# Modulation sums moved from GpSimd to VectorE, and a layer's high parts multiplied ahead of its low parts

## The reference, cut to what matters

```
cond = silu(c)                                        # 1024 numbers
for i in range(4):
    shift, scale, gate = split(cond @ ada_w[i] + ada_b[i], 3)    # ada_w[i]: 1024 x 3072
    h = rmsnorm(x, norm_g[i]) * (1 + scale) + shift
    y = mixer_i(h)            # h @ w_in, attention, (o * silu(gate')) @ w_out
    x = x + gate * y
```

## Time and profile before

| | us |
|---|---|
| median of 3 runs | 2717.4 (2715.82 to 2725.14) |
| profiled execution | 2716.97 |
| its span, first to last instruction | 2715.2 |
| PE busy | 2407.9 (89%) |
| PEld busy | 1833.5 (68%) |
| DVE busy | 1598.5 (59%) |
| ACT busy | 765.6 (28%) |
| POOL busy | 915.3 (34%) |
| mean granted TensorE clock | 0.921 of full speed |

### The profile page before, as it was taken

The page is one execution under the profiler, slowest core; times in us unless marked ns, Lnnn a source line. Parts: engine busy times, 40 slices in busy tenths (PEclk is TensorE's granted clock), DMA queues, the critical chain, the costliest instruction groups (busy, mean ns, idle before and its releaser), DMA issues.

```text
span 2715.2 us, 31261 instructions
## 1 busy us (share of the span) xinstructions
PE 2407.9 (89%) x12233; PEld 1833.5 (68%) x12233; DVE 1598.5 (59%) x2435; ACT 765.6 (28%) x1706; POOL 915.3 (34%) x944
## 2 busy tenths in 40 slices
PE   3969898788999899799969989999998997999988
PEld 2756676567987666677747776577677685757666
DVE  7786674763235566664664557674745445958373
ACT  2233202512001355224331233221402215232231
POOL 2873897387800345781120010401302001040030
PEclk6979898798678899899989999999999999999999
DMA  6440455044543100441011211121121121213111
GB/s 213 140 132 8 117 135 129 1 116 117 127 78 62 32 1 3 123 116 63 32 58 59 71 48 63 32 78 63 47 93 63 62 63 33 62 47 93 47 62 62
DMA packets 229157, 200.27 MB, mean 74 GB/s; under 512 B 86835, under 2 KB 213139, under 8 KB 228755
## 3 DMA queue, kind: packets, MB, share of 16 engines
q1 hardware_dynamic: 217491, 156.33, 20.6%
q0 software_dynamic: 11520, 41.95, 5.2%
HBM read 196.16 MB, written 2.10 MB: 73 GB/s over the span
## 4 chain that ended last, share of the span: by engine, by line
PE 57%; POOL 17%; DVE 17%; ACT 5%; issue 3%; DMA 0%; SPq 0%; DVEq 0%; ACTq 0%; POOLq 0%
PE bank L506 13%; PE bank L507 13%; PE bank L508 13%; POOL mix L2220 6%; POOL mix L2217 4%; PE bank L618 4%; DVE wring_parts L1515 3%; PE bank L654 3%; POOL mix L2223 2%; PE bank L632 2%; POOL mix L2204 2%; DVE whi_parts L1514 2%; PE bank L818 2%; DVE qb L1959 1%; PE bank L572 1%
## 5 line engine op out<-in xcount | busy, mean ns | idle before, releaser
L507 PE MATMUL bank<-h_parts,whi_parts 128*128 128x512 f32 (+2 forms) x1336 | 539.5, 404 | 0.0
L1515 DVE TENSOR_TENSOR wring_parts<-wring,whi_parts 128x2048 fp32r<-128x2048 f32 (+1 forms) x138 | 326.4, 2365 | 4.7
L1514 DVE CAST whi_parts<-wring 128x2048 fp32r<-128x2048 f32 (+1 forms) x138 | 192.3, 1394 | 201.5 <-PE bank L508 167.1
L507 PEld LDWEIGHTS bank<-h_parts,whi_parts 128*128 128x128 f32 (+2 forms) x1336 | 253.6, 190 | 69.2 <-issue 5.9
L2220 POOL TENSOR_TENSOR mix<-mix 128x512 f32<-128x512 f32 (+1 forms) x160 | 214.5, 1341 | 12.5
L506 PE MATMUL bank<-vt_parts,whi_parts 128*128 128x512 f32 (+2 forms) x472 | 199.9, 424 | 18.1 <-POOL h_parts L2251 12.1
L507 PE MATMUL bank<-mix_parts,whi_parts 128*128 128x512 f32 x512 | 202.9, 396 | 0.0
L506 PE MATMUL bank<-pt_parts,whi_parts 128*128 128x512 f32 x392 | 166.3, 424 | 36.7 <-DVE wring_parts L1515 20.9
L508 PE MATMUL bank<-vt_parts,wring_parts 128*128 128x512 f32 (+2 forms) x472 | 190.4, 403 | 0.0
L1586 DVE CUSTOM_DVE_ANT_0 bank<-bank,causal 128x128 f32<-128x128 f32 (+3 forms) x256 | 120.2, 512 | 76.0 <-PE bank L618 75.6
L618 PE MATMUL bank<-kb,qb 64*128 64x128 f32 (+3 forms) x1024 | 156.7, 385 | 8.7 <-ACT pr L1199 4.0
(11 more groups left out here) (375 smaller groups left out, 5363.9 us busy)
## 6 DMA issues: line engine op xcount, KB each, us to landing
wring<-in_w_in SPq DMA_DIRECT2D x60, 1024.0 KB, 5.2
mix<-in_ada_w POOLq DMA_DIRECT2D x80, 512.0 KB, 4.6
wring<-in_w_out SPq DMA_DIRECT2D x16, 1024.0 KB, 5.1
wring<-in_mla_w_in SPq DMA_DIRECT2D x10, 1024.0 KB, 7.0
wring<-in_mla_w_out SPq DMA_DIRECT2D x8, 1024.0 KB, 5.2
wring<-in_swa_w_in SPq DMA_DIRECT2D x32, 256.0 KB, 4.7
wring<-in_nsa_w_in SPq DMA_DIRECT2D x32, 256.0 KB, 4.5
wring<-in_nsa_w_in SPq DMA_DIRECT2D x6, 1024.0 KB, 5.2
```

The lines of the kernel that those rows point to most:

```text
L507: pe.matmul(bank, lh, rl, start=False, stop=False)
L1514: chain(dve.tensor_copy(high, whole))
L1515: dve.tensor_tensor(low, whole, high.bitcast(F32), ALU.subtract).then_inc(done, 1)
```

## The change

GpSimd's sums go. Its `ada_loads` starts the loads alone: a load is now two row chunks of 512 columns (512 KB as before), and from the third on it waits until the rows of the load two before are summed. VectorE's `ada_rows(more)` sums the next rows as `weighted_rows` does, one 128 by 512 instruction a row, 16 rows a part, 160 in all; it is called behind gates (4 rows each in layer 0, else 2), behind the q ropes of layers 1 and 2 (2 each) and behind the residuals of y0 to y4 (3, 3, 3, 3, 4) in layers 0 to 2. The modulation of part 3L+4 moves on TensorE from behind y7 to ahead of y6, and on VectorE to ahead of `residual(L, 6)`. `tables(1)` moves behind the `prepare` that follows `constants()`. `first_blocks` makes the four products with the high part of h as soon as this is there, and the two with the low part two chunks later (LOW_LAG). It holds for all six layers.

```diff
...
 AHEAD = 2
+LOW_LAG = 2
...
                 b = [open_bank(A, key) for key in keys]
-                for k in range(KC):
-                    right = hk(k)
-                    for j in range(2):
-                        mm = product(b[j][:, :], [t[:, k, j * P:(j + 1) * P] for t in by_chunk(slots)], right, k == 0, k == KC - 1)
-                        if k == KC - 1:
-                            mm.then_inc(A.full, 1)
+                unseen[0] = 0
+                for step in range(KC + LOW_LAG):
+                    if step < KC:
+                        pe.wait_ge(*cnt(h_kept))
+                        for j in range(2):
+                            high, low = [t[:, step, j * P:(j + 1) * P] for t in by_chunk(slots)]
+                            pe.matmul(b[j][:, :], high, hh[step], start=(step == 0), stop=False)
+                            pe.matmul(b[j][:, :], low, hh[step], start=False, stop=False)
+                    k = step - LOW_LAG
+                    if k >= 0:
+                        pe.wait_ge(*cnt(h_ready))
+                        for j in range(2):
+                            high = by_chunk(slots)[0][:, k, j * P:(j + 1) * P]
+                            mm = pe.matmul(b[j][:, :], high, h_parts[:, k, :], start=False, stop=(k == KC - 1))
+                            if k == KC - 1:
+                                mm.then_inc(A.full, 1)
...
-                pe.wait_ge(*(cnt(start_summed, 2) if n < 2 else cnt(ada_summed)))
+                pe.wait_ge(*(cnt(start_summed, 2) if n < 2 else (ada_step, 2 * KC * (n - 1))))
                 bank = open_bank(V, ("ada", L, part))
...
                 for i in range(4):
+                    if L + 1 < len(LAYERS) and i == 3:
+                        modulation(L + 1, 1)
                     keys = [(L, "y", 2 * i + j) for j in range(2)]
...
                 out_proj(L, 1)
-                if L + 1 < len(LAYERS):
-                    modulation(L + 1, 1)
             norm_x(4)
...
+            summed = [0]
+
+            def ada_rows(more):
+
+                for _ in range(more):
+                    n, at = divmod(summed[0], 2 * KC)
+                    half, k = divmod(at, KC)
+                    u, n = KC * (n + 2) + at // 2, n + 2
+                    summed[0] += 1
+                    if k % 2 == 0:
+                        dve.wait_ge(ada_loaded[u % 2], 16 * (u // 2 + 1 - KC))
+                    t = ada_ring[:, u % 2, S * (k % 2):S * (k % 2 + 1)]
+                    to = acc[:, n % 2, S * half:S * (half + 1)]
+                    if k == 0:
+                        dve.wait_ge(*V.filled(("ada",) + todo[n - 2]))
+                        dve.tensor_scalar(to, t, cond[:, 0:1], None, ALU.mult).then_inc(ada_step, 1)
+                    else:
+                        dve.scalar_tensor_tensor(out=to, in0=t, scalar=cond[:, k:k + 1], in1=to, op0=ALU.mult, op1=ALU.add).then_inc(ada_step, 1)
+                    dve.wait_ge(*cnt(ada_step))
+
             def tables(source):
...
                 chain(dve.tensor_reduce(inv[:, :], invsel[:, :], AX.X, ALU.add))
-                tables(1)
...
                         gate((L, "gate", b), mix[:, b, :])
+                        ada_rows(2 if L else 4)
                         if b == 1 and L:
...
                     if L == 0:
+                        tables(1)
                         dve.wait_ge(*cnt(tables_act, 3))
...
                         rope((L, "q", b), scale)
+                        ada_rows(2)
                         if b % 2:
                         gate((L, "gate", b), mix[:, b, :])
+                        ada_rows(2)
                         if b in (1, 3):
...
                         rope((L, "q", b), scale)
+                        ada_rows(2)
                         if b % 2:
...
                             gate((L, "gate", 2 * i + j), mix[:, 2 * i + j, :])
+                            ada_rows(2)
                         if i < 2:
...
                 for b in range(KC):
+                    if b == 6 and L + 1 < len(LAYERS):
+                        modulation(L + 1, 1)
                     residual(L, b)
                         prepare()
+                    if b < 5 and L + 1 < len(LAYERS):
+                        ada_rows(3 if b < 4 else 4)
                 add_square(L + 1, KC - 1)
                 prepare()
-                if L + 1 < len(LAYERS):
-                    modulation(L + 1, 1)
             norm_apply(4, lambda k: col("final_norm_g", k), x, x_normed)
...
-            def modulation(n):
...
+            asked = [2 * KC]
+
+            def ada_loads(n, ahead):
+
+                for u in range(asked[0], min(KC * n + ahead, KC * len(todo))):
+                    L, part = todo[u // KC]
+                    w = a["ada_w"][L].rearrange("(k p) n -> p k n", p=P)
+                    k, c = 2 * (u % 4), part * D + S * (u % KC // 4)
+                    if u >= 2 * KC + 2:
+                        pool.wait_ge(ada_step, 2 * (u - 2 * KC - 1))
+                    pool.dma_start(ada_ring[:, u % 2, :].rearrange("p (k n) -> p k n", k=2), w[:, k:k + 2, c:c + S]).then_inc(ada_loaded[u % 2], 16)
+                    asked[0] = u + 1
...
                 low_parts(L)
-                modulation(3 * L + 2)
-                if L + 1 < len(LAYERS):
-                    modulation(3 * L + 3)
+                ada_loads(3 * L + 4, 2)
                 if LAYERS[L] == "nsa":
...
                 normalise(L)
-                if L + 1 < len(LAYERS):
-                    modulation(3 * L + 4)
+                ada_loads(3 * L + 5, 2)
...
```

More of the change, by code:

```diff
@@ L241, in mix_high @@
             return [qb_parts[:, k, :] for k in range(KC)]
+        todo = [(L, part) for L in range(len(LAYERS)) for part in range(3)]
         def squares_of(n):
@@ L267, in program @@
         gate_done = sem("gate_done")
-        cond_tanh, cond_ready, ada_step, ada_summed = sem("cond_tanh"), sem("cond_ready"), sem("ada_step"), sem("ada_summed")
+        cond_tanh, cond_ready, ada_step = sem("cond_tanh"), sem("cond_ready"), sem("ada_step")
         small_normed, lat_split = sem("small_normed"), sem("lat_split")
@@ L2194, in _ @@
             pool.iota(pcol[:, :], [[0, 1]], base=0, channel_multiplier=1).then_inc(consts_ready, 1)
-            todo = [(L, part) for L in range(len(LAYERS)) for part in range(3)]
-            parts_done = []
-            def ada_load(n, r):
-                L, part = todo[n]
-                u = KC * n + r
-                w = a["ada_w"][L].rearrange("(k p) n -> p k n", p=P)
-                c = part * D + r * P
-                pool.dma_start(ada_ring[:, u % 2, :].rearrange("p (k n) -> p k n", k=KC), w[:, :, c:c + P]).then_inc(ada_loaded[u % 2], 16)
@@ L2206, in modulation @@
-            def modulation(n):
-                if n == 2:
-                    ada_load(2, 0)
-                    ada_load(2, 1)
-                    pool.wait_ge(*cnt(cond_ready))
-                pool.wait_ge(*V.filled(("ada",) + todo[n - 2]))
-                for r in range(KC):
-                    u = KC * n + r
-                    t = ada_ring[:, u % 2, :].rearrange("p (k n) -> p k n", k=KC)
-                    pool.wait_ge(ada_loaded[u % 2], 16 * (u // 2 + 1 - KC))
-                    pool.tensor_tensor(t, t, cond[:, :, None].to_broadcast([P, KC, P]), ALU.mult).then_inc(ada_step, 1)
-                    for width in (4, 2):
-                        pool.wait_ge(*cnt(ada_step))
-                        pool.tensor_tensor(t[:, 0:width], t[:, 0:width], t[:, width:2 * width], ALU.add).then_inc(ada_step, 1)
-                    pool.wait_ge(*cnt(ada_step))
-                    last = ada_summed if r == KC - 1 else ada_step
-                    pool.tensor_tensor(acc[:, n % 2, r * P:(r + 1) * P], t[:, 0], t[:, 1], ALU.add).then_inc(last, 1)
-                    pool.wait_ge(*cnt(last))
-                    nn, rr = (n, r + 2) if r < KC - 2 else (n + 1, r + 2 - KC)
-                    if nn < len(todo):
-                        ada_load(nn, rr)
```

## The result

The changed kernel takes 2695.0 us (median of 4 runs, 2693.7 to 2697.1) against 2717.5 before; ratio 0.9917, 95% interval 0.9899 to 0.9934. It is faster by 22 us, less than half of the 51 forecast; the time lies inside the range. The span of the profiled execution went from 2715.2 to 2693.8 us, TensorE's mean granted clock from 0.921 to 0.928. One execution of the experiment mod_last ran in a slow state (3226.9 us at a granted clock of 0.68) and is left out of its ratio; its median without it is 2672.7 us.

The account below looks back on a forecast made before the run. GpSimd was taken to cost twice: TensorE waits for its modulation sums, and it slows VectorE beside it. Terms 21 + 4 + 17 + 9 + 8 - 11 = 48, plus 3 allowance: 2717 - 51 = 2666 us; 8-in-10 range 2644 to 2698.

Parts of the forecast that it names:

- (b): First blocks, high parts first: products start 1.9 us sooner; 4 us (0 to 5) counted for the second stack's two layers.
- (a): Layer 0 ahead of attention: quiet VectorE and tables moved behind kv_b's split start attention at 175.5 instead of 196.53, 21 us.
- (c): Tails of layers 0, 1, 2: waits ahead of the norm go, less small products and a 3 us stall; 17 us (14 to 27).
- (d): Layer 1 ahead of attention: TensorE's 8.87 us wait for GpSimd goes; 9 us, 4 if splits come late.
- (e): Layer 3 ahead of attention: VectorE's ropes and splits run at quiet durations, TensorE's clock stays up; 8 us (3 to 8).
- (f): Layer 2: a loss, softmax maskings queue on GpSimd behind loads that wait for rows; -11 us (-6 to -14).
- allowance: VectorE's other stretched splits, in layer 0's last attention unit and layer 2's first blocks: 3 us, between 0 and 6.
- Rival 1: The two-slot load ring starves VectorE: each us of landing over 4.6 costs 17 us, up to 2763 us; chance 0.05.
- rival 2: The tails give little: a stall of 8 us instead of 3 makes 2681; chance 0.20, together with smaller gains up to 2709.

Follow-up runs that it names:

- mod_last: Also experiment 1: the changed kernel with the modulation put back behind y7, the rows staying where they are; 2673.3 us, ratio 0.9845.
- experiment 2: Also rows_ahead: the changed kernel, modulation still mid-tail, four of its sixteen rows summed earlier, ahead of attention's last output unit; 2677.7 us, ratio 0.9856.
- Experiment 3: The changed kernel with each load of modulation rows after the first two bringing 128 instead of 512 columns; 2676.7 us, ratio 0.9838.
- experiment 6: The changed kernel, layer 0 only: key blocks copied out ahead of sine and cosine, last two query swaps behind the value blocks; 2697.9 us, ratio 0.9942.
- experiment 5: Also tables_back: the changed kernel with VectorE's table work back ahead of kv_b's split in layer 0; 2701.8 us, ratio 0.9936.
- experiment 7: The changed kernel with the first two blocks of each layer in the order of the kernel before; 2708.6 us, ratio 0.9981.
- gps_busy: The changed kernel with twelve extra GpSimd multiplications on a dead buffer, in layer 0's tail and ahead of layer 1's attention; 2720.6 us, single execution.
- combined: The changed kernel with modulation behind y7, layer 2's loads between maskings, layer 0's key blocks copied ahead of sine and cosine; 2665.0 us, ratio 0.9808.
- experiment 4: The changed kernel with GpSimd's loads in layer 2 issued between its maskings, the last two behind the last masking; 2694.0 us, ratio 0.9924.

## Why the prediction was wrong

Direction and range were right, the size was not: 22 us (21.4 in the spans) for 51. By its own steps, in us; (b)'s share of other layers lies in (a) and (c), as in the prediction:

| step | forecast | measured |
|---|---|---|
| (a) layer 0 ahead of attention | 21 | 11.3 |
| (b) first blocks, second stack | 4 | 0.2 |
| (c) tails of layers 0 to 2 | 17 | 3.5 |
| (d) layer 1 ahead of attention | 9 | 7.7 |
| (e) layer 3 ahead of attention | 8 | 6.9 |
| (f) layer 2 | -11 | -8.9 |
| allowance; attention of layers 0, 1, 3 and the rest | 3 | 0.7 |

(The measured (c) is -4.0 in the tails and 2.8 + 2.8 + 1.9 from the norm to the next first product: 9.53 us before in all three, now 6.70, 6.70 and 7.65. (d), (e) and (f) count from that product.)

**The step that failed is (c)**, in the sentence "Paid: the modulation's 16 small products stand in the middle of TensorE's work, 1.84 us at full clock, and TensorE waits there for row 16." The stall was sized right, 3.6, 3.8 and 3.7 us against 3 (0 to 4). Its price was not. I let TensorE resume at full speed; after the stall the products took 3.57 us and y6's first twelve products ran at half speed, a clock of 0.76 over 18 us. Three times 1.7 and 2.7 us (experiment 2) are 13.2, against the 13.5 that (c) falls short. The rows to see it in were before me: 3.80 us of waiting and then 2.30 us for the same products, 10.76 and then 3.57, and the 0.65 of the earlier trace rows. Experiments 1 and 2 show both halves: leave the products where they are but without a stall, and the tails are 7.7 to 9.1 us shorter; put them behind y7, and it is 1.7 more. The same term explains why the tail of layer 0 got slower than before (56.8 for 53.3), although a 3.80 us wait ahead of the norm had gone: it was traded for one in the middle of the work.

The Trainium skill, "TensorE: Matmul & The Clock Gate", in its section on HAM oscillation, describes that rule: a wait lets the gate throttle TensorE, and what comes next starts cold. The trace agrees: 3.57 us for the products behind the wait of 3.60, 1.84 without one. The prediction reckoned with it for the norm's product and not for this place.

**(a), second in size.** kv_b's split ended 5.2 us late: the first gate ran at 98.2 instead of 96, and VectorE's waits for loads, put at 2.5 us for each of four pairs, 10, were 13.8. The other 4.5 us lie behind the split. Experiment 3 prices the waits: with 7.2 us of them attention starts at 177.7, 2.2 from the forecast. Another part is ScalarE: sine and cosine stood between TensorE and its banks (the 5.28 us wait), while the prediction let the copies follow them without holding TensorE; experiment 6 gave 3.4 to 4.2 back. The tables' move itself is worth nothing (experiment 5). The two small modulations stand in series in front of attention with 3.63 us.

**(b).** In the first stack the 1.9 us show as 0.7 to 2.2 ahead of each attention (experiment 7). In the second stack the first blocks did end earlier, by 0.8 us in layer 4 and 1.6 in layer 5, 2.4 for the forecast's 4; the clock behind them undid it. Layer 5 takes 673.4 us from its norm to the end for 670.0 before and 669.9 in the old order. That is no chance of one execution: from layer 5's first norm to its second, all twelve profiles with the new order take 375.6 to 375.7 us and both with the old one 372.1 to 372.2. Layer 4 took 668.6 us from norm to norm for 672.3 before and 672.7 in the old order, but four of the twelve with the new order (rows_ahead, tables_back, gps_busy, combined) took 671.4 to 672.0, so most of that gain is not the order's.

Most of layer 5's loss can be seen behind one wait of TensorE. First the kernel after, time line and the 20 us from the wait's end, then the one with the old order:

```profile
2337.70 3.68 PE L1009 MATMUL bank<-ident,qb 128*128 128x128 f32 x16 [3.03 <-DVE qb L2009]
```

```profile
2337.70:2357.70 20.00, 19.89 (x64) 13.43 (x65) 13.47 (x35) 3.51 (x9) 6.71 (x8) 0.78 0.00 1
```

```profile
2355.40 3.29 PE L999 MATMUL bank<-ident,qb 128*128 128x128 f32 x16 [3.03 <-DVE qb L1999]
```

```profile
2355.40:2375.40 20.00, 19.92 (x73) 12.56 (x74) 13.66 (x35) 5.63 (x14) 7.63 (x9) 0.93 0.11 30
```

The same wait of 3.03 us, and a clock of 0.78 in one and 0.93 in the other. Why an edit far ahead of it changes the clock there is open.

**Right** were the price of a row (0.78 us from start to start, four in 3.11), the quiet durations, (d), (e), and (f) with its mechanism, 8.9 us for 11; experiment 4 gave 4.5 to 5 us of it back. Rival 1 had the right place, the ring, with a smaller effect; rival 2 named the right stage and priced it by the stall alone.

## What to carry to other kernels

A wait of TensorE in the middle of dense work can cost the wait and, behind it, time at half clock: here 3.7 us of waiting with sixteen small products behind it cost 8 to 9, and behind a wait of 1.62 us with full products after it the clock stayed up. Price it from rows of the same kind, and put an operand that comes late where TensorE waits anyway. Before a chain is moved off one engine, follow the ring that feeds it: VectorE waited 13.8 us for loads ahead of layer 0's attention, and what was queued behind the loads in layer 2 cost another 4.5 to 5.

## What the runs showed of the hardware

GpSimd's arithmetic costs VectorE its own duration, one to one, where an instruction of VectorE that has its operands in SBUF (seen for the split's subtraction and the ropes) falls beside it: 18.7 us for 19.1. In the kernel before the cast and the gates grow too (1.23 to 2.34 us for the cast, ahead of layer 1's attention). An instruction that reads a bank ran beside GpSimd 19 times in the kernel before and stayed at 0.69 us.

A stall of 0.97 us with sixteen products of one column behind it let the granted clock fall; the same products without a stall did not, nor did a wait of 1.62 us with full products behind it.

The granted clock can differ by several us a stage where the instructions are the same. Layer 2 from attention's first product to its output projection, in the kernel after and in mod_last:

```profile
889.80:1064.50 174.70, 154.24 (x1442) 109.11 (x1443) 110.57 (x394) 94.24 (x304) 76.21 (x128) 0.95 0.01 1
```

```profile
871.20:1051.40 180.20, 159.59 (x1441) 112.06 (x1442) 110.52 (x394) 94.49 (x304) 76.70 (x128) 0.92 0.01 1
```

In fourteen profiles it took 174.4 to 175.3 or 179.6 to 180.4 us and nothing between. Two executions of the kernel after differ by 3.2 us in layer 0's attention and 2.1 in layer 1's, so part of this comes with the execution; in layer 5, as above, it comes with the program. So an edit worth less than 5 us is better read from its stage than from the total.
